# Weight slots at four different addresses modulo 512 bytes, low activations 64 bytes beyond the high ones

## What is computed

```
first block:   h += 0.5 * swiglu(norm(h), w_gate, w_up, w_down)      # 1024 -> 2*2816 -> 1024
               h += concat(window_attention, gated_linear_attention) @ w_out
               h += 0.5 * swiglu(norm(h), ...)                       # a second MLP
               h += sigmoid(norm(h) @ ple_gate) * norm(p @ ple_proj)
second block:  x += even_mixer(norm(x))       # short conv + differential attention
               x += mem_attention(norm(x), norm(mem))
               x += conv_ffn(norm(x))         # gated MLP with a width-3 conv
               x += odd_mixer(norm(x))        # stick-breaking attention
               x += mem_attention(...);  x += conv_ffn(...)
```

## Time and profile before

| What | Value |
|---|---|
| Time, median of 2 runs | 2561.93 us (2561.89 to 2561.97) |
| Profiled execution: span from the first to the last instruction | 2561.3 us |
| Busy: PE / PEld / DVE / ACT / POOL | 2541.6 / 2107.0 / 1596.4 / 912.6 / 10.2 us |
| Matmuls and loads of a stationary operand | 12548 of each |
| DMA | 241.91 MB, mean 94 GB/s |

### The profile page before, as it was taken

How to read it: one execution, slowest core, us unless ns; L and a number is a source line. 1 busy time by engine, 2 the same in 40 slices (tenths; PEclk the granted TensorE clock), 3 DMA queues, 4 the chain that set the end, 5 groups by cost and what they waited for, 6 DMA issues and landing times.

```text
span 2561.3 us, 31974 instructions
## 1 busy us (share of the span) xinstructions
PE 2541.6 (99%) x12548; PEld 2107.0 (82%) x12548; DVE 1596.4 (62%) x1976; ACT 912.6 (36%) x1184; POOL 10.2 (0%) x24
## 2 busy tenths in 40 slices
PE   8999999999999999999999999999999999999999
PEld 7888888778888888877898888888886888888887
DVE  6444468866444468677765747476357665775755
ACT  5222234543222245344443423233146343432322
POOL 0000001000000000000000000000000000000000
PEclk9999999999999999999999999999999999999999
DMA  5222233112222232212321232323210232232222
GB/s 182 102 83 99 96 110 120 67 50 96 103 89 98 99 115 101 99 50 99 132 94 63 104 103 82 115 83 123 94 66 13 87 116 83 84 115 83 101 96 82
DMA packets 37410, 241.91 MB, mean 94 GB/s; under 512 B 4416, under 2 KB 7280, under 8 KB 9136
## 3 DMA queue, kind: packets, MB, share of 16 engines
q1 hardware_dynamic: 34736, 233.78, 26.3%
q10 hardware_dynamic: 1920, 5.22, 0.6%
q0 software_dynamic: 640, 1.31, 0.2%
HBM read 236.89 MB, written 2.10 MB: 93 GB/s over the span
## 4 chain that ended last, share of the span: by engine, by line
PE 93%; DVE 5%; ACT 1%; issue 1%; DMA 0%; POOL 0%; DVEq 0%; ACTq 0%
PE ps L605 24%; PE ps L607 24%; PE ps L606 24%; PE ps L1234 1%; PE ps L623 1%; PE ps L625 1%; PE ps L624 1%; PE ps L766 1%; PE ps L1267 1%; PE ps L1291 1%; PE ps L1282 1%; DVE w_lo L2048 1%; PE ps L768 1%; PE ps L767 1%; PE ps L1303 1%
## 5 line engine op out<-in xcount | busy, mean ns | idle before, releaser
L605 PE MATMUL ps<-op_hi,w_hi 128*128 128x512 f32 x2056 | 800.9, 390 | 0.2 <-DVE op_lo L1929 0.2
L606 PE MATMUL ps<-op_lo,w_hi 128*128 128x512 f32 x2056 | 800.5, 389 | 0.0
L607 PE MATMUL ps<-op_hi,w_lo 128*128 128x512 f32 x2056 | 800.4, 389 | 0.0
L1350 ACT ACTIVATE w_hi<-w_raw 128x2048 fp32r<-128x2048 f32 x217 | 414.4, 1911 | 485.2 <-PE ps L607 315.3
L2048 DVE TENSOR_TENSOR w_lo<-w_raw,w_hi 128x2048 fp32r<-128x2048 f32 x217 | 497.0, 2292 | 38.7 <-ACT w_hi L1350 22.3
L605 PEld LDWEIGHTS ps<-op_hi,w_hi 128*128 128x128 f32 x2056 | 386.3, 188 | 81.4 <-issue 1.4
L607 PEld LDWEIGHTS ps<-op_hi,w_lo 128*128 128x128 f32 x2056 | 386.2, 188 | 80.6
L606 PEld LDWEIGHTS ps<-op_lo,w_hi 128*128 128x128 f32 x2056 | 386.3, 188 | 80.3
L2013 DVE SCALAR_TENSOR_TENSOR x<-ps,x 128x512 f32<-128x512 f32 x134 | 92.7, 691 | 310.8 <-PE ps L607 293.0
L605 PE MATMUL ps<-h_hi,w_hi 128*128 128x512 f32 x692 | 269.5, 389 | 0.0
L606 PE MATMUL ps<-h_lo,w_hi 128*128 128x512 f32 x692 | 269.2, 389 | 0.0
(11 more groups left out here) (373 smaller groups left out, 3085.7 us busy)
## 6 DMA issues: line engine op xcount, KB each, us to landing
w_raw<-in_wstream_dram SPq DMA_DIRECT2D x217, 1024.0 KB, 4.8
cr_m<-in_mem_dram ACTq DMA_DIRECT2D x2, 1024.0 KB, 4.9
w_raw<-in_wstream_dram SPq DMA_DIRECT2D x7, 256.0 KB, 8.0
x<-in_x_dram SPq DMA_DIRECT2D x3, 512.0 KB, 7.3
out_dram<-x SPq DMA_DIRECT2D x3, 512.0 KB, 2.6
m_s<-m_q POOLq DMA_DIRECT2D x16, 64.0 KB, 2.5
ev_s<-in_alibi_dram ACTq DMA_DIRECT2D x1, 1024.0 KB, 4.9
m_c<-in_rope_dram ACTq DMA_DIRECT2D x1, 640.0 KB, 3.9
```

Source lines behind the costliest of these rows:

```text
L605: mm_(o, w_hi[:, c % 4, w], hi[:, k, 0:cols], start=(k == 0), stop=False)
L606: mm_(o, w_hi[:, c % 4, w], lo[:, k, 0:cols], start=False, stop=False)
L607: mm = mm_(o, w_lo[:, c % 4, w], hi[:, k, 0:cols], start=False, stop=(k == kt - 1))
L1350: f_(w_hi[:, c % 4, :], w_raw[:, c % 2, :], ACT.Copy).then_inc(w_hi_ready, 1)
```

## The change

The weight slots are made 16 bytes longer (`SLAB + 4` elements, of which the last 4 are unused), so slot s begins 16 x s bytes beyond slot 0 modulo 512. Unused tensors are put between the large ones: 64 bytes before `op_lo`, and 448 bytes before `w_hi`, before `w_lo` and before the tensors that start at `h_hi`. By their sizes `op_lo` begins at 192 modulo 512, slot s of `w_hi` and of `w_lo` at 128 + 16 x s, and all that follows keeps its place modulo 512. Together this takes 1,536 bytes more in each partition. The space reserved for dynamic transfers is set to 8,192 bytes, half of what it was, which moves everything by a multiple of 512. No instruction, wait or transfer is added, removed or moved.

```diff
--- before.py
+++ after.py
@@ -167,9 +167,13 @@
             od_hi = sb("od_hi", [P, 2, TRI], FP32R, s)
 
         op_hi = sb("op_hi", [P, KT, SEQ], FP32R)
+        sb("fill_op", [P, 16])
         op_lo = sb("op_lo", [P, KT, SEQ], FP32R)
-        w_hi = sb("w_hi", [P, 4, SLAB], FP32R)
-        w_lo = sb("w_lo", [P, 4, SLAB], FP32R)
+        sb("fill_w", [P, 112])
+        w_hi = sb("w_hi", [P, 4, SLAB + 4], FP32R)[:, :, 0:SLAB]
+        sb("fill_w_lo", [P, 112])
+        w_lo = sb("w_lo", [P, 4, SLAB + 4], FP32R)[:, :, 0:SLAB]
+        sb("fill_h", [P, 112])
 
         with ExitStack() as s:
             h_hi = sb("h_hi", [P, 8, SEQ], FP32R, s)
@@ -2956,7 +2960,8 @@
     import concourse.bacc as _bacc
     from concourse.bass_utils import run_bass_kernel_spmd as _run
 
-    nc = _bacc.Bacc("TRN2", target_bir_lowering=False, num_devices=1)
+    nc = _bacc.Bacc("TRN2", target_bir_lowering=False, num_devices=1,
+                    dynamic_dma_scratch_size=8192)
     arrays, args = {}, {}
     for name, a in lay_out({k: np.asarray(v) for k, v in inputs.items()}).items():
         arrays[f"in_{name}_dram"] = np.ascontiguousarray(a)
```

## The result

| What | Before | After |
|---|---|---|
| Time, median of 2 runs | 2561.93 us | 2606.49 us (2606.17 to 2606.82) |
| Ratio, with its 95% interval | | 1.0172 [1.0156, 1.0189] |
| Span of the profiled execution | 2561.3 us | 2604.4 us |

The kernel became 1.7% slower: 15.5 us above the forecast of 2591 us, inside the range, and on the side that the forecast named. The page of after has the same numbers of instructions on every engine as the earlier trace rows and the same clock; of the engines only TensorE is busy for clearly longer.

The account below looks back on a forecast made before the run. TensorE was taken as the bound: number of matmuls times spacing between starts. Slot 2 +15.2, slots 1 and 3 +15.2, 256 columns -0.9 sum to +29.5 us, giving 2591 us; 8-in-10 range 2492 to 2623.

Parts of the forecast that it names:

- TensorE bounds the kernel, and the spacing of 9096 matmuls is what the change acts on: FP32R matmuls with 512 columns: 9096 at 226.7 ns are 2062 us, of which placement could win 121 us at most.
- I take it that the place within 64 bytes is what counts, and cost this part at 0: Low activations moved 64 bytes on, seen alone in slot 0: no cost, 0 us.
- the sign that it was wrong in kind: Any shifted slot's slab under 10.88 us, or most of all slot 0 changing from 10.88 us.
- Slot 2, 233.3 ns: Weight slot 32 bytes off, priced from `embeddings`: +6.7 ns on each of 2274 matmuls, +15.2 us.
- Slots 1 and 3, half the price: Weight slots taken as 16 bytes off: +3.3 ns on each of 4548 matmuls, +15.2 us.
- 256 columns, -0.9 us: `to_positions` and its cut form, shifted in three slots, gain 0.9 us; cross attention's keys and values 0, at most 2 us.
- Halved reserved space, 0: Space for 20 GpSimd transfers, first mixer's window only: no cost, about 10 us as upper end.
- ACT's and DVE's writes, 0: Writes to a row pitch of 8,208 bytes instead of 8,192, off the chain: no cost.
- Rival 1: 512-column matmuls start earlier when operands are shifted: 2487 to 2516 us; chance 0.33.
- Rival 2: Sixteen bytes are too few to matter, or each slot finds the rhythm again: 2562 us; chance 0.17.
- Rival 3: All slots, slot 0 too, lose the rhythm at the price of `embeddings`: +61 us, 2622 us; chance 0.15.

Follow-up runs that it names:

- the scans: Two kernels: weight slots and `h` moved in the kernel before, reserved space halved, to cover 16 operand distances; 2596.92 and 2612.02 us, one run each.

## Why the prediction was right, and where its steps failed

*TensorE bounds the kernel, and the spacing of 9096 matmuls is what the change acts on: right.* These matmuls carry +45.0 us, and all the other matmuls together -1.4; no other engine's busy time moved by more than 0.8 us, and clock and bytes are the same.

*"I take it that the place within 64 bytes is what counts, and cost this part at 0": wrong.* This is the step that failed. Alone, the 64 bytes cost 32.4 us, and slot 0 went from 10.88 to 11.12 us, which the prediction itself had named as the sign that it was wrong in kind. The error was in the reading of the earlier trace rows: `sums_hi` lies 256 bytes from the tiles before it, and I took from its undisturbed spacing a period of 64, where 256 is the period that the scans show. One row can't tell 64 from 256. And `sums_r`, its own stationary operand, begins at 384 as `sums_hi` does, so in that row the matmul's own two operands were not apart at all.

*Slot 2, 233.3 ns: right in size.* 233.1 for `h` and, with the slots alone, 233.2 for `op`, from `embeddings` as the nearest row. That row was the right one for a reason I hadn't seen: its distance was 32 bytes modulo 256 (288), not only modulo 64.

*Slots 1 and 3, half the price: mis-sized, both.* Alone, slot 1 costs next to nothing (1.6 us) and slot 3 the full price (13.9), so their sum came out near my 15.2 us by luck. Cost isn't a line through the distance; it goes by whole rhythms.

*Slot by slot, as it came out together* (mine, then measured, `op` and `h`): slot 0 0 and +7.6 us, slot 1 +7.6 and +14.2, slot 2 +15.2 and +14.1, slot 3 +7.6 and +9.4. The missing 15 us are slots 0 and 1, which the low activations' step should have carried. That the parts don't add kept the time inside the range: their sum would have been 2624 us, just above it. Of the 32.4 us left out, 17.5 came back because the two parts together cost less than apart, which no term of mine had foreseen; that much of the hit is luck.

*256 columns, -0.9 us: right in sign,* -1.9 measured, and +0.9 in the cross attention, within the 2 us allowed.

*Halved reserved space, 0: right,* by the run with everything 32 bytes on. *ACT's and DVE's writes, 0: right,* by the windows of after, in which DVE is busy for 5.49 us of an `op` slab and ACT for 2.44, as before.

*The rivals.* Rival 1 (the shift frees the rhythm) is out for 512 columns at all distances tried. Rival 2 (nothing) is out. The Trainium skill's rule that would have given it (SBUF — State Buffer, section "Who interferes with whom": the two reads of TensorE wait for nobody) isn't borne out for these products: only places changed, and a slab went from 10.88 to 11.29 us. Which of the two reads waits, and for what, no trace here shows. Rival 3 (lost everywhere) is nearest in kind: slot 0 is lost too. Its price of 233.3 throughout was too high for `h`, which keeps 227 in two slots, and for `op` in slots 0 and 3, and too low for `op` in slot 1.

## What to carry to other kernels

Where FP32R matmuls of 512 columns follow one another, let the moving and the stationary operand of every one begin at the same place modulo 256 bytes, to the element, the low parts of a split product included; here nearly every other choice cost 0.7 to 3.7% of each matmul. Measure a placement by windows of one slab, slot by slot, and more than once in the kernel: one place can run in several rhythms, and parts of such a change don't add up. Before a row of the trace is made a rule ("within 64 bytes"), ask which other rules it would fit as well.

## What the runs showed that was not expected

- Products at the same distances ran in two or three rhythms within one execution, and a rhythm lasted until other matmuls came between. With the low activations 128 bytes on, these rhythms are whole steps of 6.67 ns a trio apart (slabs of 10.99, 11.09 and 11.20 us, against 10.88 in before).
- A shift of 4 bytes of the weight slot costs 5.8 ns a matmul (232.5), one of 16 bytes 0.3 (227.0 for `h`; 0.9 more than before for `op`, 227.9).
- One matmul in three out of place lengthens the whole trio. With the low weights moved as well, one and two out of place cost the same (231.2 ns), and one alone at 64 bytes (232.0) costs more than all three at 64 (229.2).
- With 256 columns the match is not the best: 119.8 to 120.9 ns at distance 0, 113.3 to 117.8 at 192. How to hold the 113.3 is open; over 768 matmuls it would be worth some 3 us more, an estimate from 768 x 4.5 ns.
